# Down-projection weights of a quad's last two experts loaded and multiplied by column halves, in the second mixture of experts of a two-block kernel

## The reference, cut to what matters

```python
def hier_moe(v, w_grp, b_grp, w_exp, b_exp, w_gate, w_up, w_down):
    ...
    combine = jnp.einsum('tk,tke->te', w, jax.nn.one_hot(expert_id, MOE_N_EXPERTS, dtype=f32))
    y = jnp.zeros(vt.shape, f32)
    for e in range(MOE_N_EXPERTS):
        hdn = jax.nn.silu(vt @ w_gate[e]) * (vt @ w_up[e])
        y = y + (combine[:, e:e + 1].astype(hdn.dtype) * hdn) @ w_down[e]
```

## Time and profile before

| | us |
|---|---|
| median of 3 runs | 2004.33 |
| lowest and highest | 2003.74, 2004.73 |
| the profiled execution | 2002.11 |
| span of its trace | 2000.4 |
| TensorE (PE) busy, matmuls | 1904.5 (95% of the span) |
| the second experts, first gate matmul to the end of the span | 1553.98 to 2000.4 |

### The profile page before, as it was taken

One profiled execution on the slowest core, in us unless ns is written; L12 is line 12 of the kernel. 1 busy time (PEld: TensorE's weight loads), 2 busy tenths in 40 slices (PEclk: granted clock), 3 DMA queues, 4 the chain that ended last, 5 costly groups with the idle time before them and its releaser, 6 DMA issues. The chain is left out here.

```text
span 2000.4 us, 24337 instructions
## 1 busy us (share of the span) xinstructions
PE 1904.5 (95%) x10042; PEld 878.1 (44%) x10042; DVE 524.1 (26%) x1057; ACT 358.2 (18%) x655; POOL 133.1 (7%) x210
## 2 busy tenths in 40 slices
PE   8999999999999999999999999999999998988888
PEld 6688667433333333333333333345455333333233
DVE  4588535321221212221212122232433100000001
ACT  1755412100000000000000000124441111001111
POOL 2532220000000000000000000100020000000000
PEclk9999999999999999999999999999999999999999
DMA  9974623999999999999999999945356999999997
GB/s 334 365 251 156 218 98 156 400 426 421 428 427 429 429 428 428 429 429 428 428 429 429 428 428 429 409 152 176 103 205 234 401 428 427 427 429 429 428 429 321
DMA packets 110072, 712.57 MB, mean 356 GB/s; under 512 B 14682, under 2 KB 34532, under 8 KB 72376
## 3 DMA queue, kind: packets, MB, share of 16 engines
q1 hardware_dynamic: 110008, 711.67, 87.0%
HBM read 710.55 MB, written 1.10 MB: 356 GB/s over the span
## 5 line engine op out<-in xcount | busy, mean ns | idle before, releaser
L2105 PE MATMUL ps<-ring,arena 128*64 128x512 f32 x1536 | 337.2, 593 | 9.8 <-DMA ring<-in_moe_w_gu 9.8
L2105 PEld LDWEIGHTS ps<-ring,arena 128*64 128x64 f32 x1536 | 109.0, 137 | 231.9 <-issue 208.5
L3420 PE MATMUL ps<-ring,arena 128*32 128x512 f32 x768 | 172.8, 615 | 20.5 <-DMA ring<-in_w_gate 18.5
L2135 PE MATMUL ps<-ring,arena 128*64 128x512 f32 x768 | 168.9, 592 | 0.0
L2167 ACT ACTIVATE arena<-arena 128x512 f32<-128x512 f32 x32 | 20.2, 630 | 754.6 <-DVE arena L2203 754.6
L2594 PE MATMUL ps<-ring 128*128 128x512 f32 (+1 forms) x320 | 137.6, 579 | 0.7 <-ACT ring L2989 0.6
L2105 PE MATMUL ps<-arena 128*64 128x512 f32 x512 | 113.2, 593 | 3.3 <-DMA arena<-in_moe_w_gu 3.3
L1381 PEld LDWEIGHTS ps<-arena 128*128 128x128 f32 x832 | 96.0, 192 | 34.5 <-issue 32.7
L3420 PEld LDWEIGHTS ps<-ring,arena 128*32 128x32 f32 x768 | 45.5, 113 | 139.9 <-issue 139.0
L2203 DVE TENSOR_SCALAR arena<-ps 128x512 f32<-128x512 f32 x32 | 22.1, 691 | 314.3 <-PE ps L2105 314.3
L1381 PE MATMUL ps<-arena 128*128 128x128 f32 x832 | 104.0, 280 | 0.2
(11 more groups left out here) (624 smaller groups left out, 2074.0 us busy)
## 6 DMA issues: line engine op xcount, KB each, us to landing
ring<-in_moe_w_gu SPq DMA_DIRECT2D x96, 2048.0 KB, 25.4
ring<-in_moe_w_down SPq DMA_DIRECT2D x48, 2048.0 KB, 28.3
arena<-in_moe_w_gu SPq DMA_DIRECT2D x31, 2048.0 KB, 24.1
ring<-in_w_gate SPq DMA_DIRECT2D x26, 2048.0 KB, 25.9
ring<-in_w_down SPq DMA_DIRECT2D x24, 2048.0 KB, 24.5
ring<-in_w_up SPq DMA_DIRECT2D x22, 2048.0 KB, 30.4
ring<-in_w_in SPq DMA_DIRECT2D x19, 2048.0 KB, 11.3
arena<-in_moe_w_down SPq DMA_DIRECT2D x15, 2048.0 KB, 30.8
```

The costliest lines, as they stand in the source:

```text
L2105: last = M.matmul(ps[halves[j], 4 + which, :], xgT[buf][:, k, CAP * ee:CAP * ee + CAP], w[k2][:, at:at + 512], start=(first and k == 0), s ...
L2135: last = M.matmul(ps[halves[j], 6, :], yT[:, k % KH, halves[k // KH]], w[k % KH][:, 512 * j:512 * j + 512], start=False, stop=(k == 2 * KH ...
L3420: last = M.matmul(ps[quads[e], 4 + which, :], xgT[:, k, quads[e]], w[e][k], start=(k == 0), stop=(k == KD - 1))
```

## The change

For each quad the down chunks of experts 2 and 3 are no longer loaded as one DMA of 2 MiB each. Each is loaded as a left half (columns 0 to 511 of `w_down`) and a right half (columns 512 to 1023), one DMA of 1 MiB each, in the order left of 2, left of 3, right of 2, right of 3. In a slot the left half takes the first 2048 elements of each partition and the right half the last 2048. The right halves of all quads share one semaphore, `s_right`. The bytes are the same.

On TensorE the left halves are multiplied first. Then TensorE waits for ACT's copy of that half, scatters it (two matmuls), waits for `s_right`, and multiplies the right halves. The scatter in the next quad, and the one behind the loop, then only have the right half to add: two matmuls each.

The first two refills get a wait of their own: the left halves wait for `s_half`, which TensorE sets when it has multiplied the first four of the eight rows of the first pair of gates. The right halves wait, as before, for the whole pair. `cleared.extend(spent)` moves up, so that the new semaphores have numbers to use.

```diff
--- before.py
+++ after.py
@@ -1245,7 +1245,7 @@
 
 
 
-        def __init__(self, name, chunks, count, per_done, unroll, most, spare=(), turns_in_spare=()):
+        def __init__(self, name, chunks, count, per_done, unroll, most, spare=(), turns_in_spare=(), by_columns=()):
             self.name, self.chunks, self.count, self.per_done, self.unroll, self.most = name, chunks, count, per_done, unroll, most
             self.turn = count * unroll
             assert self.turn % ESLOTS == 0 and ESLOTS % per_done == 0
@@ -1258,6 +1258,10 @@
             self.full = [sem(f"{name}_slot{n}_full") for n in range(ESLOTS)]
             self.spare_full = [sem(f"{name}_spare{n}_full") for n in range(len(spare))]
             self.s_done = sem(f"{name}_slots_multiplied")
+            self.by_columns = by_columns
+            if by_columns:
+                self.s_half = sem(f"{name}_first_slots_half_multiplied")
+                self.s_right = sem(f"{name}_right_columns_loaded")
 
         def uses(self, j):
 
@@ -1268,7 +1272,19 @@
 
             src, k, w = self.chunks(item + j // self.count)[j % self.count]
             n = (j - self.shift) % ESLOTS
-            sp.dma_start(expert_slot(n, k, w), src).then_inc(self.full[n], 16)
+            if j % self.count in self.by_columns:
+                self.load_columns(sp, item, j, n, 0)
+                if j % self.count == self.by_columns[-1]:
+                    for i in range(len(self.by_columns)):
+                        self.load_columns(sp, item, j + 1 - len(self.by_columns) + i, n + 1 - len(self.by_columns) + i, 1)
+            else:
+                sp.dma_start(expert_slot(n, k, w), src).then_inc(self.full[n], 16)
+
+        def load_columns(self, sp, item, j, n, side):
+
+            src, k, w = self.chunks(item + j // self.count)[j % self.count]
+            sp.dma_start(expert_slot(n, 2 * k, w // 2)[:, k * side:k * side + k, :],
+                         src[:, :, w // 2 * side:w // 2 * (side + 1)]).then_inc(self.s_right if side else self.full[n], 16)
 
         def load_spare(self, sp, j):
             src, k, w = self.chunks(j // self.count)[j % self.count]
@@ -1303,8 +1319,23 @@
                     self.load_spare(sp, j)
                 else:
                     gone = self.in_ring[self.in_ring.index(j) - ESLOTS]
-                    sp.wait_ge(self.s_done, gone // self.per_done + 1)
-                    self.load_ring(sp, j)
+                    at = self.in_ring.index(j) % ESLOTS
+                    if j in self.by_columns:
+                        if j == self.by_columns[0]:
+                            sp.wait_ge(self.s_half, 1)
+                            for i, c in enumerate(self.by_columns):
+                                self.load_columns(sp, 0, c, at + i, 0)
+                        sp.wait_ge(self.s_done, gone // self.per_done + 1)
+                        self.load_columns(sp, 0, j, at, 1)
+                    elif j % self.count in self.by_columns:
+                        sp.wait_ge(self.s_done, gone // self.per_done + 1)
+                        self.load_columns(sp, 0, j, at, 0)
+                        if j % self.count == self.by_columns[-1]:
+                            for i in range(len(self.by_columns)):
+                                self.load_columns(sp, 0, j + 1 - len(self.by_columns) + i, at + 1 - len(self.by_columns) + i, 1)
+                    else:
+                        sp.wait_ge(self.s_done, gone // self.per_done + 1)
+                        self.load_ring(sp, j)
 
 
             def turn(item, base):
@@ -2481,8 +2512,10 @@
                 + [(one(w_up, e).rearrange("(p k) n -> p k n", k=KD), KD, 512) for e in quad]
                 + [(one(w_d2, e).rearrange("(p k) n -> p k n", k=4), 4, 1024) for e in quad])
 
+    cleared.extend(spent)
     loads2 = ExpertLoads("experts2", gate_up_down2, 3 * QUAD, 2, 2, MAXP2,
-                         [((10752, 2048), (24576, 1024), (22720, 1024)), ((0, 2048), (4096, 2048))])
+                         [((10752, 2048), (24576, 1024), (22720, 1024)), ((0, 2048), (4096, 2048))],
+                         by_columns=(3 * QUAD - 2, 3 * QUAD - 1))
     quads = [slice(CAP2 * e, CAP2 * (e + 1)) for e in range(QUAD)]
 
 
@@ -3335,7 +3368,6 @@
 
 
 
-    cleared.extend(spent)
     gfin = ar(5120, D)
     s_p13 = sem("final_weight_loaded")
 
@@ -3392,9 +3424,9 @@
                     for half in range(2):
                         gather_half(x_tok, onehot, half, 6 + half, s_xg)
 
-                def scatter(pair, done=None):
+                def scatter(pair, done=None, sides=range(2)):
                     for t in range(T):
-                        for d in range(2):
+                        for d in sides:
                             last = M.matmul(ps[:, 2 * t + d, :], GT[pair][:, t, :], y2[:, d, :], start=False, stop=False,
                                             skip_group_check=True)
                         if done is not None:
@@ -3419,6 +3451,8 @@
                                 for e in pair:
                                     last = M.matmul(ps[quads[e], 4 + which, :], xgT[:, k, quads[e]], w[e][k],
                                                     start=(k == 0), stop=(k == KD - 1))
+                                if first and which == 0 and pair == pairs[0] and k == KD // 2 - 1:
+                                    last.then_inc(loads.s_half, 1)
                             last.then_inc(s_done, 1)
                             if pair == pairs[0]:
                                 pe.wait_ge(s_y2, i * 4 + 2)
@@ -3426,7 +3460,7 @@
                                 if which:
                                     gather(i + 1)
                                 elif turn is not None or u:
-                                    scatter(1)
+                                    scatter(1, sides=range(1, 2))
                     pe.wait_ge(s_y, i + 1)
                     for k in range(KH):
                         last = M.transpose(ps[:, 5, k * P:(k + 1) * P], y[:, k, :], ident[:, :])
@@ -3440,14 +3474,22 @@
                     last.then_inc(s_GT, 1)
                     pe.wait_ge(s_yTt, i + 1)
                     for c, pair in enumerate(pairs):
-                        w = [arrived(u, 2 * QUAD + e, turn, 4, 1024) for e in pair]
+                        if c == 0:
+                            w = [arrived(u, 2 * QUAD + e, turn, KH, 1024) for e in pair]
+                        else:
+                            w = [arrived(u, 2 * QUAD + e, turn, 2 * KH, 512) for e in pair]
                         for d in range(2):
+                            if c and d:
+                                pe.wait_ge(s_y2, i * 4 + 5)
+                                scatter(1, sides=range(1))
+                                pe.wait_ge(loads.s_right, i * 32 + 32)
                             for k in range(KH // 2):
                                 for n, e in enumerate(pair):
                                     for h in range(2):
                                         r = 2 * h + k
-                                        last = M.matmul(ps[quads[2 * n + h], (4, 7)[d], :], yT[:, r, quads[e]],
-                                                        w[n][r][:, 512 * d:512 * (d + 1)], start=(k == 0), stop=(k == KH // 2 - 1))
+                                        rows = w[n][KH * d + r] if c else w[n][r][:, 512 * d:512 * (d + 1)]
+                                        last = M.matmul(ps[quads[2 * n + h], (4, 7)[d], :], yT[:, r, quads[e]], rows,
+                                                        start=(k == 0), stop=(k == KH // 2 - 1))
                             if d == 0:
                                 last.then_inc(s_dh, 1)
                         last.then_inc(s_done, 1)
@@ -3466,7 +3508,7 @@
 
                 pe.wait_ge(s_GTt, n * NQ + 1)
                 pe.wait_ge(s_y2, n * (4 * NQ) + 2)
-                scatter(1, s_added)
+                scatter(1, s_added, range(1, 2))
 
             @block.scalar
             def _(act):
```

## The result

The changed kernel takes **2011.41 us** (median of 7 runs, 2010.08 to 2013.44) against 2004.33 before (7 runs, 2000.58 to 2006.19): a ratio of 1.004, 95% interval 1.003 to 1.005. It is slower by some 7 us. The forecast was 2010.1, in a range from 2003.2 to 2012.6. Rivals B and C, at 2012.2, lie somewhat nearer to the measured time than the forecast does.

What follows compares the result with a forecast made beforehand. From first refill to last landing, the stage was taken as one long DMA transfer of 86 chunks. +7.3 - 3.2 + 1.1 + 0.6 = +5.8 us on 2004.33 gave 2010.1 us, range 2003.2 to 2012.6.

Steps and rivals of the forecast that it cites:

- rival B: Down chunk loads: short runs cost more, 1.4 us a quad, +7.9 us in all, 2012.2 us; chance 0.11.
- Rival C: First refill: the change brings no head start, `s_half` no earlier or DMAs behind it waiting; +7.9, 2012.2 us; chance 0.04.
- Step 1: Down chunk loads: 2 KB runs load at 387 GB/s, not 428; 1.04 us a quad, seven quads, +7.3 us.
- Rival A: Down chunk loads: short runs cost little here; sum -0.5 us, 2003.8, or +2.6, 2006.9 at half price; chance 0.20.
- Step 2: First refill: left halves issued at about 1557.6, not 1561.09, closing the whole DMA gap; -3.2 us.
- Step 3: Refill of quad 1's third and fourth up chunks: released later by quad 0's longer last step, pausing the transfer; +1.1 us.
- Step 4: Tail, from quad 7's first gates: chain bound by TensorE, with one more round trip to ACT; +0.6 us.

Runs made afterwards that it cites:

- short_runs: Kernel before, with the down chunks of experts 2 and 3 of each quad loaded as column halves in 2 KB runs, no head start; 2012.96 us, ratio 1.0053.
- long_halves: Changed kernel, with each half DMA taking two of a partition's four weight rows (one 8 KB run), not half the columns; 2005.3 us, ratio 1.0011.
- early_rows: Kernel before, with only the first refill's two chunks loading their first two weight rows early, in 8 KB runs; 2000.71 us, ratio 0.9987.
- no_early: Changed kernel without its head start: the first refill's left halves also wait for the whole first pair of gates; 2012.03 us, ratio 1.0041.
- first_cols: Kernel before, with only the first refill's two chunks as column halves in 2 KB runs, left ones issued early; 2003.61 us, ratio 0.9999.
- no_mid_scatter: Changed kernel with the scatter back in one piece, behind the next quad's first gates and behind the loop; loads unchanged; 2007.69 us, ratio 1.0024.
- row_halves: Kernel before, with halves by weight rows (8 KB runs) in every quad, early first refill, whole scatter, last down projection rows outermost; 2000.50 us, ratio 0.9981.
- runs_4k: Kernel before, with the down chunks of experts 2 and 3 of each quad loaded whole but in 4 KB runs; 2007.07 us, ratio 1.0016.

## Why the prediction was right, and where its sizes were off

**Step 1, short runs, +7.3: right.** 7.4 in short_runs and 7.1 by the distance between the last quads' gates (59.78 - 58.77, seven times). The rate of 387 at 2 KB, read in other layers, held in this one: 385 here. The upper bound, 1.4 a quad from `w_out` on an empty queue, was too high, and rival B with it. Rival A, that short runs cost little here, is ruled out by short_runs and long_halves.

**Step 2, head start, -3.2: the step that was mis-sized.** The early issue came as foretold, 3.67 us after the first gate matmul. With long runs it is worth 2.96 (early_rows). In the changed kernel it is worth 389.89 - 390.68 = -0.79, and -0.79 - 0.86 = -1.65 with the pause of step 3 set aside. (That takes it that no_early has no pause; its gates of quad 7 stand within 0.13 of those of short_runs, which has the refill in time.) I had argued that the new halves show data 1.0 us after their issue, before the old chunks end, and that "the whole gap closes". That 1.0 us came from long runs on an empty queue. The changed kernel has 201 and 227 GB/s in two slices instead, 1.0 us lost, and first_cols has a like hole. The second loss was not in the prediction at all: it took the mean rate for the landing of a chunk, and the last of the 16 parts lies 0.85 us further behind the mean in no_mid_scatter (1.89) than in no_early (1.04). Rival C, the head start isn't there, comes close in size (+7.9) by another cause: `s_half` came early and nothing waited behind it.

**Step 3, the late refill, +1.1: right in kind, 0.9 in size.** The refill is 2.84 us later than before (2.63 foretold), and the gates of quad 7 lose 0.86 by it (no_mid_scatter). Of this 0.55 shows in the mean of the parts and 0.31 in their drift. The hole itself, 1603 to 1606, is only 0.6 us at 427. That the chunks ahead lasted longer because the head start was smaller would fit it, with 1.9 us in long_halves as the other end; it was not tested by itself.

**Step 4, the tail, +0.6: right, +0.84, and partly by luck.** The second square starts 57.77 after the gates of quad 7, where it was 57.03. Two terms of mine are off and cancel in part. I let the chain gain 0.4 at the first up pair, because I read its start before as 1957.41. That row has 29 of the 32 records; the first of them stands earlier, right at the landing:

```profile
1956.95 0.59 PE L3420 MATMUL ps<-arena 128*32 128x512 f32 x1
```

This is 19.57 after the gates, and 19.58 in the changed kernel (1967.42). So nothing is gained there, and from the end of the first pair's scatter to the second square it takes 0.80 more than before, where I had 1.0. But I read the step as the price of the change as a whole. It is the price of the split scatter alone: with the scatter whole, the same loads give an end that is 0.88 shorter than before.

**The sum:** 7.41 - 1.65 + 0.86 + 0.84 = 7.5, and the trace has 7.33. The forecast was 5.8; the 1.5 between them is the head start. The measured time is inside the range because the other steps held, and the range was wide enough for this one.

## What to carry to other kernels

Where a stage is one long transfer, look at how long the contiguous runs of each DMA are before cutting it for the sake of an earlier start: cut along the dimension that keeps the runs long (here weight rows, by a new assignment of rows to matmuls), not across it. Issue early the one transfer that ends a hole in the queue, in long runs, and leave the others whole. Count a gain where the last part of the chunk lands, and not in bytes moved. Before work is put between two halves of a product, check that the engine isn't already on the path there, and who waits for the slot that it frees later.

## What the runs showed of the hardware that I had not expected

**Each run has a price, and it is about the same at every length.** A chunk of 2 MiB is 128 KB for each of the 16 engines, and a quad has two such chunks: 16 runs of 16 KB an engine, 32 of 8 KB, 64 of 4 KB, 128 of 2 KB. By the distance between the last quads' gates (58.77 before, 58.89 in row_halves, 59.21 in runs_4k, 59.78 in short_runs) the prices are 0, 0.12, 0.44 and 1.01 us a quad, that is 8, 9 and 9 ns for each added run. I had no row for 4 and 8 KB runs with a full queue and had not looked for a price at 8 KB, which took most of what row_halves could have gained on early_rows.

**A head start in bytes is not a head start in landings.** The last of a chunk's 16 parts lands 1.0 to 1.3 us behind their mean in before, early_rows, no_early and short_runs, and 1.9 to 2.2 behind it in the three kernels where short runs are issued early; row_halves, early with 8 KB runs, lies between (1.7). The spread from the first part to the last, at the gates of quad 7, is 2.2 us before and 3.2 to 3.9 there. It came up in steps within the first 130 us of the stage and stayed. Why is open.

The Trainium skill (DMA: Bandwidth & Descriptors, Why small descriptors are slow) gives a fixed overhead of about 3 cycles for each packet beside 1 for each 32 B. The form, a fixed price for each packet, agrees with these runs. The size does not: an estimate by it gave 0.40 us a quad at 2 KB, the runs 1.01. And 2 KB is well over the 512 B that the same page (Specifications) asks for at line rate.

**Issuing short runs can hold up SP.** In the changed kernel and in the kernel before, SP's issues of down chunks in the second experts (min, median, max in ns):

```profile
L1286 SPq DMA_DIRECT2D ring<-in_w_down x32: 540/630/16184, 1561.6 to 1983.4; - x32
```

```profile
L1271 SPq DMA_DIRECT2D ring<-in_w_down x12: 332/355/378, 1781.1 to 1958.5; - x12
```

One issue took 16 us, where 378 ns was the longest in the loop before. It goes with the short runs: in short_runs the longest is 16.8 us, and in long_halves, with as many DMAs in 8 KB runs, 433 ns. SP could not issue the gates behind it until then: at 1906.71 the four halves take 19.46 us together. It cost nothing that these traces show: the rate from 1710 to 1948 stayed at 421, at a DMA share of 1.01.
